# The v half of a gMLP product first, its gate inside the u half, and the first norm tile by tile

## What is computed

```python
def rms_norm(x, g):
    return x * lax.rsqrt(jnp.mean(x * x, axis=-1, keepdims=True) + RMS_EPS) * g

def gmlp_mixer(h, w_uv, sgu_gain, w_s, b_s, w_o):      # h: tokens x 1024
    z = jax.nn.gelu(h @ w_uv)                          # w_uv: 1024 x 6144
    u, v = jnp.split(z, 2, axis=-1)                    # 3072 columns each
    v = rms_norm(v, sgu_gain)                          # over all 3072 columns
    return (u * chunk_spatial_gate(v, w_s, b_s)) @ w_o, v

# layer 0: h = rms_norm(x, norm_mix[0]); x = x + gmlp_mixer(h, ...); then a mixture of 16 experts
# then K and V of rms_norm(x, norm_kv), and layer 1: Q of rms_norm(x, norm_mix[1]), attention, experts
```

## Time and profile before

| what | us |
|---|---|
| median of 3 runs | 1547.96 (1546.93 to 1548.41) |
| the profiled execution | 1544.7 |
| its span, first to last instruction | 1542.9 |
| TensorE busy in the span | 1246.5 (81%) |
| VectorE, ScalarE, POOL busy | 567.9, 412.2, 168.8 |
| mean granted TensorE clock | 0.905 of full |

### The profile page before, as it was taken

How to read it: one execution, slowest core, us unless ns; L and a number is a source line. 1 busy time by engine, 2 the same in 40 slices (tenths; PEclk the granted TensorE clock), 3 DMA queues, 4 the chain that set the end, 5 groups by cost and what they waited for, 6 DMA issues and landing times. The chain is left out here.

```text
span 1542.9 us, 22257 instructions
## 1 busy us (share of the span) xinstructions
PE 1246.5 (81%) x8931; PEld 1090.5 (71%) x8931; DVE 567.9 (37%) x1008; ACT 412.2 (27%) x861; POOL 168.8 (11%) x129
## 2 busy tenths in 40 slices
PE   1799999987999855888871999948997963888890
PEld 1799999986999755777751999924336953777770
DVE  2321223339522240111124537688665342111115
ACT  4423244442312320000013522237444240000002
POOL 0300000005000001000002017750000002000002
PEclk9899999998999957999995899958998956999995
DMA  8572322221232105888884138770551205888855
GB/s 242 218 265 82 108 84 83 82 95 50 68 106 83 55 28 212 325 323 326 326 295 156 56 126 285 246 255 28 197 185 64 75 0 221 298 321 318 320 214 203
DMA packets 113405, 270.85 MB, mean 176 GB/s; under 512 B 11094, under 2 KB 69742, under 8 KB 105134
## 3 DMA queue, kind: packets, MB, share of 16 engines
q1 hardware_dynamic: 92768, 230.77, 42.1%
q0 software_dynamic: 9424, 33.13, 5.7%
q10 hardware_dynamic: 11142, 5.96, 1.4%
HBM read 225.43 MB, written 44.40 MB: 175 GB/s over the span
## 5 line engine op out<-in xcount | busy, mean ns | idle before, releaser
L998 PE MATMUL ps<-hT_parts,wh 128*128 128x260 f32 x1152 | 326.8, 284 | 0.0
L1144 PE MATMUL ps<-U,ring 128*128 128x128 f32 x2048 | 240.6, 279 | 44.5 <-DVE U L1604 44.5
L1144 PEld LDWEIGHTS ps<-U,ring 128*128 128x128 f32 x2048 | 234.8, 194 | 52.1 <-issue 33.5
L1366 DVE TENSOR_TENSOR ring_parts<-ring,wh 128x1024 fp32r<-128x1024 f32 x104 | 136.6, 1315 | 263.0 <-ACT wh L710 263.0
L996 PE MATMUL ps<-x_parts,wh 128*128 128x260 f32 x768 | 219.6, 286 | 8.7 <-ACTq L749 7.9
L998 PEld LDWEIGHTS ps<-hT_parts,wh 128*128 128x128 f32 x1152 | 218.5, 190 | 0.0
L997 PE MATMUL ps<-x_parts,ring_parts 128*128 128x260 f32 x768 | 217.3, 283 | 0.0
L996 PE MATMUL ps<-V_parts,wh 128*128 128x260 f32 x512 | 147.8, 289 | 8.2 <-DVE U_parts L1482 5.2
L996 PEld LDWEIGHTS ps<-x_parts,wh 128*128 128x128 f32 x768 | 145.3, 189 | 9.1 <-ACTq L749 8.0
L997 PE MATMUL ps<-V_parts,ring_parts 128*128 128x260 f32 x512 | 146.5, 286 | 0.0
L997 PEld LDWEIGHTS ps<-x_parts,ring_parts 128*128 128x128 f32 x768 | 145.2, 189 | 0.0
(11 more groups left out here) (250 smaller groups left out, 1757.1 us busy)
## 6 DMA issues: line engine op xcount, KB each, us to landing
ring<-in_w_e_gate SPq DMA_DIRECT2D x32, 1024.0 KB, 5.0
ring<-in_w_e_up SPq DMA_DIRECT2D x32, 1024.0 KB, 7.7
ring<-in_w_e_down SPq DMA_DIRECT2D x32, 1024.0 KB, 8.6
ring<-in_w_uv SPq DMA_DIRECT2D x24, 1024.0 KB, 5.6
U<-slots_dram SPq DMA_DIRECT2D x32, 512.0 KB, 5.7
slots_dram<-U SPq DMA_DIRECT2D x32, 512.0 KB, 8.9
ring<-in_cache_k SPq DMA_DIRECT2D x32, 512.0 KB, 4.4
ring<-in_cache_v SPq DMA_DIRECT2D x32, 512.0 KB, 5.2
```

Source lines behind the costliest of these rows:

```text
L998: ins = pe.matmul(to, wh[:, chunk % 2, c, :], rhs_l(c, half), start=False, stop=last and c == DC - 1)
L1144: ins = pe.matmul(ps[:, 2 + q, f * SLOTS:(f + 1) * SLOTS], w[:, c, (f % 2) * P:(f % 2 + 1) * P], xsT[:, q, c, :], start=c == 0, stop=c == ...
L1366: e.tensor_tensor(low_parts(b, half), w, plain(wh[:, chunk % 2]), ALU.subtract).then_inc(split_lo, 1)
```

## The change

- The products of v run first, then those of u; block order and ring stay. All loops over chunks are written out.
- The gate of chunk j runs beside the products of u: the spatial product of v's chunk j+1 stands behind u's product j on TensorE, through PSUM banks 4 to 7; VectorE applies gain and bias in place in PSUM (`gate`), multiplies it into gelu(u) in `vtmp`, ScalarE makes the high part of the product (`u_high`) and VectorE the low part (`u_low`). u no longer has a place of its own. POOL no longer multiplies; it loads the bias of one group at a time into two buffers.
- In place of the spatial matrices v itself is scaled by its norms, in place, between the halves. v is stored by chunks.
- The sample rows of v are transposed back behind six of the spatial products.
- The first norm goes by tiles: square on VectorE, root on ScalarE, reciprocal, scaled copy, transposes, evictions, one tile behind the other. The rows of w_uv, and of w_q, w_k and w_v, are taken in another order, so that the scaled copies of the first norm and of that ahead of Q, K and V read x without a step.
- The gains of that norm, of the Q norm and of the K, V norm, and that of v, are loaded as rows and transposed by TensorE. ScalarE issues only these three loads and the identity; SP issues the rest behind x and the first two weight blocks.
- The tables are staged in u's place in place of v's, and made behind the 12th product of v.

```diff
@@ SP
+            w_uv = a["w_uv"][0].rearrange("(c p) n -> p c n", p=P)
...
+            def uv_load(k):
+                at = (k + DG // 256) % (2 * DG // 256) * 256
+                load(UV0 + k, w_uv[:, :, at:at + 256], (DC, 256))
             for k in range(RING):
+                if k == 2:
+                    small_loads()
+                uv_load(k)
@@ POOL
+            for q in range(NG):
+                if q == 0:
+                    g.wait_ge(uv_sq, GC)
+                if q >= 2:
+                    g.wait_ge(gate_tmp, 3 * (q - 1))
+                g.dma_start(bsg[:, q % 2, :], a["b_sgu"][0, q:q + 1, :].broadcast_to([P, P])).then_inc(ld_bg[q % 2], 16)
             g.wait_ge(mm, done(GOC - 1))
...
-                g.tensor_tensor(u[:, j, 0:SEQ], gtmp[:, j % 4, :], u[:, j, 0:SEQ], ALU.mult)\
-                    .then_inc(gate_u, 1)
...
+            g.wait_ge(gate_fr, GC + len(VS_AFTER))
+            g.wait_ge(gate_u, GC)
             for t in range(5):
...
                 g.dma_start(x[0:rows_of(t), t, :], src).then_inc(again_x, 16)
@@ ScalarE
+            def u_high(j):
+                s.wait_ge(gate_u, j + 1)
+                s.wait_ge(gate_fr, spatial_at(j) + 1)
+                s.wait_ge(gate_sp, spatial_at(min(j + 1, GC - 1)) + 1)
+                s.activation(uh[:, j, :], vtmp[:, j % 2, :], ACT.Copy).then_inc(u_hi, 1)
+
+            for c in range(GC):
+                if c >= 2:
+                    s.wait_ge(uv_ev, c - 1)
+                gelu(c)
+                high_after(c)
+                if c >= 1:
+                    squares(c - 1)
+                if c == PREP_AT:
+                    s.wait_ge(prep_lam, 1)
+                    s.activation(lam_s[:, 2:4], lam_s[:, 0:2], ACT.Exp).then_inc(prep_lame, 1)
             for j in range(GC):
...
+                gelu(GC + j)
+                high_after(GC + j)
+                if j == 0:
+                    squares(GC - 1)
+                    s.wait_ge(gate_var, 1)
+                    s.activation(gss[:, 1], gss[:, 0], ACT.Sqrt).then_inc(gate_root, 1)
+                    s.wait_ge(gate_rs, 1)
+                    for t in (1, 3):
+                        s.activation(v[:, :, t, :], v[:, :, t, :], ACT.Copy, scale=gss[:, 2, t:t + 1])\
+                            .then_inc(gate_vn_a, 1)
+                else:
+                    u_high(j - 1)
@@ TensorE
+            uv(0)
+            for n in range(1, GC + 1):
+                uv(n)
+                turn_v(n - 1)
...
             pe.wait_ge(gate_v8, 1)
+            pe.matmul(ps[:, 6, 0:GC * NB], ones, v8sq, start=True, stop=True).then_inc(gate_vt, 1)
+            uv(GC + 1)
+            uv(GC + 2)
             pe.wait_ge(gate_vn_v, 2)
             pe.wait_ge(gate_vn_a, 2)
+            pe.wait_ge(gate_var, 1)
+            for j in range(4):
+                spatial(j)
+            for j in range(3, GC):
+                uv(GC + j)
+                if j + 1 < GC:
+                    spatial(j + 1)
@@ VectorE
+            def gate(j):
...
+                e.wait_ge(gate_sp, at + 1)
+                e.wait_ge(ld_bg[g % 2], 16 * (g // 2 + 1))
+                e.scalar_tensor_tensor(bank.rearrange("p (t f) -> p t f", t=NT),
...
+                                       ALU.mult, ALU.add).then_inc(gate_tmp, 1)
+                e.wait_ge(uv_gelu, GC + j + 1)
...
+                e.tensor_tensor(vtmp[:, j % 2, 0:SEQ], bank, vtmp[:, j % 2, 0:SEQ], ALU.mult).then_inc(gate_fr, 1)
+            for c in range(GC):
+                low_after(c)
+                evac(c)
+                if c == PREP_AT - 1:
+                    prepare()
+            low_after(GC)
+            v_stats()
             for j in range(GC):
+                gate(j)
+                if j + 1 < GC:
+                    low_after(GC + j + 1)
+                u_low(j)
...
             e.wait_ge(again_x, 16 * 5)
-            for m in range(2, 3 * DC):
+            for m in range(1, 3 * DC):
```

## The result

The changed kernel takes 1502.27 us (median of 4 runs, 1499.24 to 1505.76) against 1548.18 (4 runs) of the kernel before: a ratio of 0.9705 [0.9679, 0.973]. On another chip it was 1504.16 against 1545.86, 0.9738 [0.9716, 0.9759]. The profiled execution after took 1505.76 us (span 1503.9), 38.9 less than the profiled one before; the medians lie 45.9 apart. Two executions of later kernels enter no comparison of times: one of `keep_warm`, 1601.56 us at a mean granted clock of 0.794, and one of `vector_4_more`, 3902.65 us with TensorE several times slower from its start.

What follows compares the result with a forecast made beforehand. TensorE, busy four fifths of the span, was taken as the bound, with gains only where it waits: -18.8 + 33.0 - 46.85 + 1.1 - 3.0 = -34.6 from 1544.7, so 1510.1 profiled, 1513 as median; range 1503 to 1526.

Steps and rivals of the forecast that it cites:

- Front: Start to first product: ScalarE freed of issuing, norm tile by tile; 47.55 to 28.7, -18.8 us (-16 to -22).
- Half the front: Rival at the start: x or gains land late, 9.9 us not won; 1523, chance 0.12.
- none of it: Rival at the start: nothing won at the front; 1532, chance 0.04.
- Inside the uv stretch: v and u products: TensorE pays for spatial products, transposes, a stop between the halves and its clock; +33.0 us.
- The 46.85 behind it: TensorE's idle between last uv and first w_gmlp_o product falls away if VectorE keeps up in the u half; -46.85 us.
- The rival in which it sets the pace: u half: VectorE's block stretches to 9.4 us a chunk against TensorE's 6.7; +65, 1578, chance 0.05.
- Behind the uv stretch: Ahead of the third w_gmlp_o product: late x reload, stop of 3.9 and 1.7 of clock; +1.1 us (-4.5 to +2).
- Late reload: Rival at x's reload: POOL's five issues each wait out a VectorE operation, x 3 us later; 1516, chance 0.03.
- K, V, Q norm: Norm ahead of K, V and Q: scaled copies become contiguous; -3.0 us (bounds -1.5 and -4.5).
- No stops: Rival at both TensorE stops: clock stays up and x is in time; 1506, chance 0.08.
- From profile to median: Whole kernel: the median of the runs lies 3.3 us above the profiled execution, added at the end.

Runs made afterwards that it cites:

- keep_warm: Changed kernel with 36 unread identity transposes in TensorE's stop ahead of the third w_gmlp_o product; profiled execution 1497.58 us.
- vector_4_more: Changed kernel with VectorE's low part of the gated u made five times in place of once; 1513.78 us.
- loads_on_scalar: Changed kernel with thirteen small loads and the page table issued by ScalarE again, ahead of its part of the first norm; 1521.17 us.
- vector_8_more: Changed kernel with VectorE's low part of the gated u made nine times in place of once; 1573.26 us.
- both: Changed kernel with VectorE's wait for reloaded x moved later and the sample rows of v squared ahead of a low part; 1495.88 us.
- late_wait: Changed kernel with VectorE's wait for reloaded x moved to just ahead of the first addition to x; 1498.82 us.
- kvq_contig: Kernel before with only the w_q, w_k, w_v row order and contiguous scaled copies in the norm ahead of Q, K, V; 1535.45 us.

## Why the prediction was right in kind and 11 us too high

The time, 1502.27, lies 10.7 below the predicted 1513 and 0.7 below the range's lower end. The bounding was right: two idle places, both won, at a price inside the uv stretch. Two steps failed: the 3.3 us added from profile to median, and the price inside the uv stretch. By the steps:

- **Front**: -18.8 predicted, -19.8 measured. Tile 0 landed at 5.01, not 7.0, but the root's table load of 1.28 stood in its path; 2.85 a tile from the third on, not 3.25. The 1.9 us from the fifth reciprocal to the last eviction had no row; it took 2.5. Half the front, or none of it, is ruled out by the timeline, and by `loads_on_scalar`, which shows what it would have cost.
- **Inside the uv stretch**: +33.0 predicted, +29.3 measured. This is the step that was mis-sized most in the profile. The spatial product costs 6.63 - 5.74 = 0.89 inside the loop, not 0.98 as among its own kind in the earlier trace rows: 21.4 for 24, where 23.5 was priced. The 24 sample transposes cost 0.43 in each of six chunks: 2.6. Tables 0.9, the last turn 0.45, the stop 2.79 (3.4), the clock 1.7 as said. These add up to 29.8, 0.5 more than measured; where that went is open. So 2.1 of the 3.7 is the spatial product, and the smaller terms were each a little high as well.
- **The 46.85 behind it**: gone whole, since VectorE keeps up with 3.40 to spare in the plain chunks. The rival in which it sets the pace was right as a mechanism: at a block of 9.32 `vector_8_more` gave 1573, where the rival at 9.4 had 1578. It did not happen: the product with u took 0.69, not 1.60. That POOL was the cause of the 1.60 the trace before shows by itself, in VectorE's and POOL's timelines:

```profile
351.29 0.69 DVE L1467 TENSOR_TENSOR U<-x,U 128x512 f32<-128x512 f32 x1
```

```profile
352.72 2.50 POOL L614 TENSOR_TENSOR U<-x,U 128x512 f32<-128x512 f32 x2 [1.82 <-DVE x L1461]
```

The first of VectorE's eight multiplications fell into POOL's pause of 1.82 and took 0.69; the other seven, beside POOL's, took 1.42 to 1.81.

- **Behind the uv stretch**: +1.1 predicted, +1.9 measured (23.6 against 21.7). The stop was where it was placed, for the reason given, 4.65 instead of 3.9: from the last gate step's end to the landing of x it was 9.8 (350.96 to 360.80), priced as 9.0.
- **Late reload**: POOL's five issues took 2.65 beside a VectorE that had little to do, and 2.72 in the earlier trace rows beside one that had no pause. The issues took no longer beside the busy VectorE.
- **K, V, Q norm**: -3.0 predicted, -3.0 measured; alone, -2.7.
- **No stops**: it did not happen in this kernel, but `both` comes near it, with one stop of 1.25 left, at 9.0 less in the profile; the rival had 7.3, without the 1.5 that `both` takes off the first stop.
- **From profile to median**: this failed. The working added 3.3, because before's profiled execution lay 3.3 under its median. After, the profiled one lay 3.5 above its median. The 3.3 was no property of the kernel but of one execution: over the runs here the profiled one lies from 6.0 under its median (`late_wait`) to 7.4 above (`kvq_contig`). Unrounded the forecast was 1513.4, so 11.1 too high: 6.8 of that is this step, 3.9 the terms above (1.0 + 3.7 - 0.8), and the rest stretches priced as unchanged. The range's lower end, too, was built from the terms' bounds alone and left this spread out.

The stretch behind the first experts gave 1.6 more than its norm; it differs by 2.5 among kernels with the same code there (382.6 to 385.1), so nothing is made of that.

## What to carry to other kernels

Look at what an engine issues before its first work: here small loads took up to 4 us each of its instruction stream. SP took them behind x and two weight blocks, and TensorE waited for none of them. Work of one engine can be hidden inside the loop of the engine that bounds it, at the price that the bounding engine pays for its own share; measure the room by adding dummy work, in the densest iterations as well as in the plain ones. Put a wait just ahead of the instruction that needs it, and ahead of other work what another engine stands waiting for: here one wait and one operation, each a few lines too early, cost 9 us together, about a third of it in clock. Where two engines multiply side by side, look at the time of one operation with and without the other.

## What was not expected of the hardware

- Issuing one of the loads ahead of the first product took from 0.30 to 4.13 us of the issuing engine's time, and the shape of the load doesn't decide it. The column of `b_sgu` took 4.01 from ScalarE in `loads_on_scalar` and 0.58 from SP in the kernel after; there `lam_q` took 3.12 and `lam_k`, of the same shape, 0.76. What decides it the runs don't show. Timeline of SP, kernel after:

```profile
5.08 4.13 SPq L478 DMA_DIRECT2D K<-in_geometry  x1
...
18.45 0.58 SPq L492 DMA_DIRECT2D w<-in_b_sgu  x1
19.08 3.12 SPq L492 DMA_DIRECT2D U<-in_lam_q  x1
22.24 0.76 SPq L492 DMA_DIRECT2D U<-in_lam_k  x1
```

- TensorE's clock fell to 1.2 GHz behind stops of 2.79, 3.54 and 4.65 us, and not behind one of 1.25; identity transposes in a stop held it at 1.00.
- One VectorE multiplication of 128x512 took 0.69 us with POOL standing still and up to 1.81 beside a multiplication on POOL.
- The same norm ran at 1.2 GHz for its whole length in one execution and rose to 2.4 within it in another, worth 6 us each time.
